# Gated recurrence of a streaming encoder: one program block over thirds of the tokens, with 64-row products of head pairs

## The chip, the core and the metric

The kernel runs on one core of one Trainium2 chip. Five engines work side by side and are tied together by semaphores: TensorE (PE in the rows; its weight loads are PEld), VectorE (DVE), ScalarE (ACT), GpSimd (POOL) and SyncE (SP), which here issues the DMA transfers. Products go into PSUM, eight banks of 512 fp32 columns on 128 partitions. The metric is device time in microseconds of one execution; less is better.

## What is computed

A trunk of two layers for 1024 prompt frames and 32 sample frames (1056 tokens). The part in question is head group A of layer 0, gated linear attention with 4 heads, 64 key and 128 value dimensions:

```python
loga = log_sigmoid(lr @ w_a2 + b_a) / 16                 # (T, 4 heads, 64)
# per chunk:  b = cumsum(loga) in the chunk
att   = einsum('thd,shd,tshd->hts', q, k, exp(b_t - b_s)) # causal, s <= t
o     = att @ v + (q * exp(b)) @ S
S_new = S * exp(b_last) + (k * exp(b_last - b)).T @ v
# then per head:  o = rmsnorm(o, onorm) * silu(g), and o goes into the output projection
```

The prompt starts with S = 0, the sample with a given state. Both last states are outputs.

## The kernel before

All tensors lie transposed: features on partitions, tokens along the free dimension (`TOK` = 1056 columns). A chunk is `C` = 32 tokens, so there are `NCH` = 33 chunks: 32 of the prompt (`NPC`), one of the sample. `BLK` is a third of the tokens, 352 columns or 11 chunks. Two heads share the 128 partitions of a pair (64 key dimensions each), so q, k and the gate are two tiles `a` of 128 partitions.

`even_layer` (L2941) runs, one after the other, program blocks that each end with all engines meeting: `front`, `even_products` (the input projection, which leaves q, k, v, g and the gate in DRAM), then for group A

- `gla_prep` (L455): loads everything whole (1056 columns), ScalarE and VectorE form log-sigmoid, the cumulated sum per chunk (a scan that the tile `keep` restarts every 32 columns), exp(c/16) as `t` and exp(-c/16) as `l`; then q*t and k*l, each written twice with a mask that keeps one head of the pair (`of_key`), and the decays `dec`.
- `gla_scan` "p" (L93) for 32 chunks, then `gla_scan` "s" for the sample's chunk. Per chunk GpSimd copies k and q into padded tiles `kp`, `qp` (L142; per pair 128 columns, of which the heads' 32 each are filled) and v into `vst` (L147). TensorE transposes `kp` and `vst` (L165, L166), forms kp.qp (L172, 128 by 128, both pairs summed into one bank), kt.vt for the state (L183), state.qp (L187) and vt.g (L190) for the output. VectorE masks (L209), adds to and decays the state (L213, L217). ScalarE empties the transposes (L229, L231) and the output (L235).
- `gla_post` (L520): per head over all 1056 columns: square (L562), column sums through a product with ones (L550), ln (L571) and exp (L574) for 1/rms, silu of g (L576), and on VectorE the gain (L583) and the gate (L587). After each the function table of ScalarE may be loaded anew (ACT_TABLE_LOAD).

Then `after_mixer` starts with the output projection's weights (L879) and everything downstream, which is untouched.

The order inside `gla_scan` comes from `staggered`: `ahead(c+1)` before `body(c)` on PE, DVE and ACT. What ties the loop: GpSimd may refill `qp` only after the output of the chunk before the last has left the array, since

```python
pe.wait_ge(y_done, c + 1)      # L191, end of scan(c) on PE
pe.sem_inc(used, 1)            # L192
pool.wait_ge(used, c + 1)      # L149, before heads(qp, q, q_padded)
```

and `make` waits for `q_padded` before L172. A product of fp32 operands is two passes on TensorE, so one product counts as x2 in the trace's rows.

## Time and profile before

| what | us |
|---|---|
| time, median of 3 runs | 3828.34 |
| lowest, highest | 3823.66, 3831.31 |
| the profiled execution's own time | 3826.76 |
| its span | 3825.0 |
| PE busy in it | 3488.0 (91%) |
| DVE, ACT, POOL busy | 1557.2, 1140.9, 602.9 |

The span runs from the first to the last instruction of the program; the 1.8 us between span and time lie around it. PE's share says little about one stage: in the page's 40 slices PE is at 9 tenths or more in most, and at 5 to 8 in a few, among them the fifth to the seventh (383 to 669 us), where group A lies.

### The profile page before, as it was taken

The numbers are of one execution on the slowest core, as the hardware profiler recorded it, in microseconds if no ns is written. First come the engines' busy times: TensorE is split into PE (matmuls) and PEld (weight loads), VectorE is DVE, ScalarE is ACT, GpSimd is POOL, SyncE is SP. The second block draws the span as 40 slices with busy tenths as digits, with TensorE's granted clock in tenths as the row PEclk, the third lists the DMA queues.
The fourth block names the chain that finished last, engine by engine and source line by source line (L and its number), as shares of the span: only waits on it lengthen the run. The fifth ranks groups of instructions, "written<-read, shape, count | busy, mean of one in ns | idle before, by whom it ended". The sixth has DMA issues, their size and how long they took to land. (4 is left out here: it accounts for less than half of the span.)

```text
span 3825.0 us, 61773 instructions
## 1 busy us (share of the span) xinstructions
PE 3488.0 (91%) x26489; PEld 3283.9 (86%) x26489; DVE 1557.2 (41%) x2522; ACT 1140.9 (30%) x2121; POOL 602.9 (16%) x859
## 2 busy tenths in 40 slices
PE   8899586999999999998899894775999999999998
PEld 8898465998999999996598784673998999999997
DVE  6345433334332232235326658456334332232233
ACT  6223225223321121124535521443323321121123
POOL 2000040101110010111312347330200210010012
PEclk9999797999999999998899997887999999999999
DMA  7322202200211111113646665965210111111111
GB/s 228 98 64 61 85 4 64 83 28 28 45 49 45 45 47 48 45 42 113 220 153 207 225 171 120 228 147 119 70 46 23 45 45 50 45 45 50 45 41 67
DMA packets 453966, 323.63 MB, mean 85 GB/s; under 512 B 105038, under 2 KB 429870, under 8 KB 450446
## 3 DMA queue, kind: packets, MB, share of 16 engines
q1 hardware_dynamic: 399450, 281.18, 25.7%
q10 hardware_dynamic: 43876, 18.99, 1.9%
q0 software_dynamic: 10368, 19.51, 1.6%
q8 instruction: 210, 3.44, 0.4%
q14 instruction: 62, 0.51, 0.0%
HBM read 232.75 MB, written 86.96 MB: 84 GB/s over the span
## 5 line engine op out<-in xcount | busy, mean ns | idle before, releaser
L83 PE MATMUL ps<-am_y,am_wh 128*128 128x352 f32 x4896 | 1178.0, 322 | 0.0
L83 PE MATMUL ps<-am_h,am_wh 128*128 128x352 f32 x3648 | 879.2, 324 | 1.2 <-DVE am_h L1379 1.2
L83 PEld LDWEIGHTS ps<-am_y,am_wh 128*128 128x128 f32 x4896 | 853.6, 188 | 1.3
L83 PE MATMUL ps<-am_y,am_wl 128*128 128x352 f32 x2448 | 789.7, 323 | 0.0
L83 PEld LDWEIGHTS ps<-am_h,am_wh 128*128 128x128 f32 x3648 | 632.1, 188 | 4.2 <-DVE am_h L1379 1.4
L83 PE MATMUL ps<-am_h,am_wl 128*128 128x352 f32 x1824 | 585.0, 321 | 0.0
L83 PEld LDWEIGHTS ps<-am_y,am_wl 128*128 128x128 f32 x2448 | 459.8, 188 | 0.0
L83 PEld LDWEIGHTS ps<-am_h,am_wl 128*128 128x128 f32 x1824 | 342.1, 188 | 0.0
L1466 POOL TENSOR_TENSOR am_silu<-am_silu,rs 128x352 f32<-128x352 f32 x132 | 126.4, 959 | 1234.4 <-ACT am_silu L1323 1234.4
L83 PE MATMUL ps<-rw_parts,rw_wh 128*128 128x352 f32 (+1 forms) x1152 | 289.3, 333 | 23.0 <-PEq L2494 13.1
L1055 DVE TENSOR_TENSOR x<-ps,x 128x352 f32<-128x352 f32 x240 | 125.8, 524 | 449.8 <-PE ps L83 439.9
L887 ACT ACTIVATE am_wh<-am_w 128x1024 fp32r<-128x1024 f32 (+1 forms) x184 | 189.4, 1030 | 377.0 <-PE ps L83 370.1
L894 DVE TENSOR_TENSOR am_wl<-am_w,am_wh 128x1024 fp32r<-128x1024 f32 (+1 forms) x184 | 222.6, 1210 | 161.6 <-ACT am_wh L887 161.6
L997 POOL TENSOR_TENSOR am_q_acc<-am_q_acc,am_q_sq 128x352 f32<-128x352 f32 x126 | 120.1, 953 | 790.2 <-ACT am_q_sq L988 790.2
L83 PE MATMUL ps<-h,ab_wh 128*128 128x352 f32 x912 | 222.7, 326 | 10.9 <-DVE ab_wl L894 10.9
L83 PEld LDWEIGHTS ps<-rw_parts,rw_wh 128*128 128x128 f32 x1152 | 202.7, 191 | 33.4 <-issue 27.1
L1438 DVE TENSOR_TENSOR am_silu<-ps,rs 128x352 f32<-128x352 f32 x132 | 69.2, 525 | 326.2 <-PE ps L83 306.8
L83 PE MATMUL ps<-rw_parts,rw_wl 128*128 128x352 f32 (+1 forms) x576 | 188.3, 327 | 0.0
L1327 ACT ACTIVATE am_h<-am_q_sq 128x352 fp32r<-128x352 f32 x132 | 65.8, 498 | 395.1 <-DVE am_q_sq L1444 395.1
L1323 ACT ACTIVATE am_silu<-am_silu 128x352 f32<-128x352 f32 x132 | 65.4, 498 | 385.3 <-DVE am_silu L1438 385.3
L83 PEld LDWEIGHTS ps<-h,ab_wh 128*128 128x128 f32 x912 | 159.1, 189 | 18.7 <-DVE ab_wl L894 11.1
L1444 DVE TENSOR_TENSOR am_q_sq<-ps,am_silu 128x352 f32<-128x352 f32 x132 | 69.2, 524 | 217.4 <-PE ps L83 217.4
(345 smaller groups left out, 4676.0 us busy)
## 6 DMA issues: line engine op xcount, KB each, us to landing
am_w<-in_ffn_w SPq DMA_DIRECT2D x120, 512.0 KB, 3.9
rw_ra_d<-tb_rk SPq DMA_DIRECT2D x8, 1056.0 KB, 8.0
rw_kbt_d<-tb_gk SPq DMA_DIRECT2D x8, 1056.0 KB, 4.0
rw_gg_d<-tb_gk SPq DMA_DIRECT2D x8, 1056.0 KB, 6.6
fr_w<-in_xa_wk SPq DMA_DIRECT2D x8, 1024.0 KB, 5.3
fr_w<-in_xa_wv SPq DMA_DIRECT2D x8, 1024.0 KB, 5.3
am_w<-in_xa_wq SPq DMA_DIRECT2D x16, 512.0 KB, 4.0
am_w<-in_xa_wo SPq DMA_DIRECT2D x16, 512.0 KB, 4.0
```

Source lines behind the costliest of these rows:

```text
L83: mm = nc.tensor.matmul(out, l, part, start=start and n == 0, stop=stop and n == 2)
L887: self.nc.scalar.activation(self.wh[:, j % 2, 0:kt], self.wt[:, j % 2, 0:kt], ACT.Copy)\
L894: self.nc.vector.tensor_tensor(self.wl[:, j % 2, 0:kt], self.wt[:, j % 2, 0:kt], whole(self.wh[:, j % 2, 0:kt]), ALU.subtract).then_inc(se ...
L997: self.nc.gpsimd.tensor_tensor(acc, acc, self.sq[:, n % 2], ALU.add).then_inc(self.added, 1)
L1055: g.frees(g.nc.vector.tensor_tensor(xs, g.bank(j, b), xs, ALU.add), j, b)
L1323: nc.scalar.activation(silu[:, columns(b)], silu[:, columns(b)], ACT.Silu).then_inc(silus, 1)
L1327: nc.scalar.activation(z[0][:, i, columns(b)], gate[:, (f + b) % 2], ACT.Copy).then_inc(highs, 1)
L1438: groups.frees(nc.vector.tensor_tensor(silu[:, columns(b)], groups.bank(j, b), rs[:, columns(b)], ALU.mult), j, b)
L1444: groups.frees(nc.vector.tensor_tensor(gate[:, (f + b) % 2], groups.bank(j + 1, b), silu[:, columns(b)], ALU.mult), j + 1, b)
L1466: nc.gpsimd.tensor_tensor(silu[:, columns(b)], silu[:, columns(b)], rs[:, columns(b)], ALU.mult)\
```

## The change

The three blocks `gla_prep`, `gla_scan` (twice) and `gla_post` become one block `gla`. In it:

- preparation goes by thirds: block b+1 of 352 columns is loaded, and its log-sigmoid (`soft`), sums (`cumulate`), exponentials (`grow`) and products (`queries` on VectorE, k*l on GpSimd) stand at fixed chunks of block b: on ScalarE after chunk 1 and 5 of a block, on VectorE after 3 and 6. `q` isn't scaled any more, the factor moves into the copy that takes the output out.
- `qp` and `kp` exist for all 33 chunks, 64 columns per pair, zeroed once; GpSimd's per-chunk copies are gone, and each third's q*t and k*l are written straight into them, a head (64 partitions) at a time.
- products of a head pair lie on 64 rows: kp.qp (L211 in the new file) is two products of 64 by 64, each on its half of rows and partitions; kv.kv (L221) takes 64 rows of each half and 128 columns; state.qp (L230) has 128 rows and 64 moving columns; kv.g (L234) 64 rows, 64 moving columns. The two transposes (L204, L205) share a bank, one copy (L365) empties it, with two banks in turn.
- the state is double (`old`, `new`), so adding doesn't overwrite what state.qp reads; the sample is chunk 32 of the same loop with states 2 and 3.
- norm and gate of third b-1 stand at fixed chunks of third b: square after chunk 0, sum and ln of one head after chunks 1 to 4, exp after 6, silu after 7 on ScalarE; gain and gate after 8 and 9 on VectorE. Those of the last third come after the loop, a head at a time.

The core of the diff (new lines; removed functions are those described above):

```diff
+            def make(c):
+                s, b = c % 2, c // PB
+                if c % PB == 0:
+                    pe.wait_ge(vr_set, b + 1)
+                    pe.wait_ge(kp_set, 2 * b + 2)
+                if c >= 2:
+                    pe.wait_ge(kv_out, c - 1)
+                nc.tensor.transpose(ps[:, A + s, 0:P], kp[:, c].rearrange("r p h t -> r (p h t)"), ident[:])
+                nc.tensor.transpose(ps[:, A + s, P:2 * P], vr[:, c].rearrange("r h t -> r (h t)"), ident[:]).then_inc(turned, 1)
+                if c % PB == 0:
+                    pe.wait_ge(qp_set, 2 * b + 2)
+                if c:
+                    pe.wait_ge(g_out, c)
+                for p, r in enumerate(halves):
+                    mm = nc.tensor.matmul(ps[r, G, 0:HD], kp[:, c, p].rearrange("r h t -> r (h t)"),
+                                          qp[:, c, p].rearrange("r h t -> r (h t)"), start=True, stop=True)
+                mm.then_inc(made, 1)
+
+            def scan(c):
+                s = c % 2
+                pe.wait_ge(kv_out, c + 1)
+                if c:
+                    pe.wait_ge(s_added, c)
+                for p, r in enumerate(halves):
+                    mm = nc.tensor.matmul(ps[:, S + p, 0:GLA_DV], kv[r, s, 0, :], kv[r, s, 1, :], start=True, stop=True)
+                mm.then_inc(s_done, 1)
+                if c == NPC:
+                    pe.wait_ge(init_in, 32)
+                else:
+                    pe.wait_ge(state_ready, c + 1)
+                if c:
+                    pe.wait_ge(y_out, c)
+                for p in range(2):
+                    nc.tensor.matmul(ps[:, Y + p, 0:HD], state[:, old(c), p, :], qp[:, c, p].rearrange("r h t -> r (h t)"),
+                                     start=True, stop=False)
+                pe.wait_ge(g_out, c + 1)
+                for p, r in enumerate(halves):
+                    mm = nc.tensor.matmul(ps[:, Y + p, 0:HD], kv[r, s, 1, :], g[r, s, :], start=False, stop=True)
+                mm.then_inc(y_done, 1)
...
+            for b in range(BLOCKS):
+                s = b % 2
+                pool.wait_ge(v_in[s], 16 * (b // 2 + 1))
+                if b == 0:
+                    pool.wait_ge(cleared, 2)
+                nc.gpsimd.tensor_copy(vr[:, chunks(b)].rearrange("p c h t -> p h c t"),
+                                      v[:, s].rearrange("p h (c t) -> p h c t", t=C)).then_inc(vr_set, 1)
+                pool.wait_ge(grown, 2 * b + 2)
+                nc.gpsimd.tensor_copy(dec[:, :, chunks(b)], by_chunk(t[:, s])[:, :, :, C - 1]).then_inc(dec_set, 1)
+                pool.wait_ge(qk_in[s], 32 * (b // 2 + 1))
+                pool.wait_ge(dec_set, b + 1)
+                for h, r in enumerate(halves):
+                    if h:
+                        pool.wait_ge(kp_set, 2 * b + 1)
+                    nc.gpsimd.tensor_tensor(kp[r, chunks(b), :, h, :].rearrange("r c p t -> r p c t"), by_chunk(k[r, s]), by_chunk(l[r, s]), ALU.mult)\
+                        .then_inc(kp_set, 1)
...
+            for c in range(NCH):
+                if c + 1 < NCH:
+                    masked(c + 1)
+                add(c)
+                b, r = c // PB, c % PB
+                if b + 1 < BLOCKS:
+                    if r == 3:
+                        cumulate(b + 1)
+                    if r == 6:
+                        queries(b + 1)
+                if b and r == 8:
+                    if b == 1:
+                        dve.wait_ge(gain_in, 16)
+                    dve.wait_ge(scales, b)
+                    norm(b - 1, 0, GLA_HEADS)
+                if b and r == 9:
+                    dve.wait_ge(normed, b)
+                    dve.wait_ge(gated, b)
+                    bend(b - 1, 0, GLA_HEADS).then_inc(done, 1)
...
         with nc.cleanup_on_exit():
-            with nc.sbuf_tensor("gla_qk", [P, 2, 2, 2, TOK], F32) as qk, nc.sbuf_tensor("gla_v", [P, 4, TOK], F32) as v:
-                q, k = qk[:, 0], qk[:, 1]
-                gla_prep(nc, ab, gate, q, k, v, dec, a["c_keep"], a["c_heads"])
-                gla_scan(nc, ps, "p", 0, NPC, q, k, v, a["c_mask_gla"], dec, ya, None,
-                         o["p_gla"][0, 0], ident)
-                gla_scan(nc, ps, "s", NPC, 1, q, k, v, a["c_mask_gla"], dec, ya, a["state_gla"][0, 0],
-                         o["s_gla"][0, 0], ident)
-            gla_post(nc, ps, ab, ya, a["gla_onorm"][0], ones)
+            gla(nc, ps, a, o, ab, gate, ya, ones, ident)
```

What stands in the queues. On PE, in the middle of the loop before, one chunk is these rows (x2: two products, one per pair):

```order
L165 MATMUL ps<-ident,glap_kp 128x128 x2
L166 MATMUL ps<-ident,glap_vst 128x128
L172 MATMUL ps<-glap_qp,glap_kp 128x128 x2
L183 MATMUL ps<-glap_vt,glap_kt 128x128 x2
L187 MATMUL ps<-glap_qp,glap_state 128x128 x2
L190 MATMUL ps<-glap_g,glap_vt 128x128
```

and in the changed kernel, same place:

```order
L204 MATMUL ps<-ident,gl_kp 128x128
L205 MATMUL ps<-ident,gl_vr 128x128
L211 MATMUL ps<-gl_qp,gl_kp 64x64 x2
L221 MATMUL ps<-gl_kv 128x128 x2
L230 MATMUL ps<-gl_qp,gl_state 128x64 x2
L234 MATMUL ps<-gl_gm,gl_kv 128x64 x2
```

One transpose fewer, one product kv.g more, and fewer moving columns in three groups (L211, L230, L234); L211, L221 and L234 take 64 rows of the array, the others 128.

On ACT, the preparation before stands whole (2112 columns: both tiles of 1056 tokens) ahead of the first chunks' copies:

```order
L484 ACTIVATE gp_t<-gp_z 128x2112
L486 ACTIVATE gp_l<-gp_t 128x2112
L489 ACTIVATE gp_t<-gp_l,gp_one 128x2112
L492 ACTIVATE gp_t<-gp_c 128x2112
L493 ACTIVATE gp_l<-gp_c 128x2112
L495 ACTIVATE gla_dec<-gp_t 128x66
```

and in the changed kernel, around the first chunks of the second third:

```order
L365 ACTIVATE gl_kv<-ps 128x256
L370 ACTIVATE o_a<-ps 128x4x32
L378 ACTIVATE gl_sq<-o_a 128x1408
L365 ACTIVATE gl_kv<-ps 128x256
L370 ACTIVATE o_a<-ps 128x4x32
L384 ACTIVATE gl_rs<-ps,gl_eps 128x352
L349 ACTIVATE gl_t<-gl_z 128x704
L351 ACTIVATE gl_l<-gl_t 128x704
L355 ACTIVATE gl_t<-gl_l,gl_one 128x704
L365 ACTIVATE gl_kv<-ps 128x256
L370 ACTIVATE o_a<-ps 128x4x32
L384 ACTIVATE gl_rs<-ps,gl_eps 128x352
```

A chunk has two copies (L365, L370) where the loop before has three (L229, L231, L235), and between them now stand the squares (L378) and ln (L384) of the first third and `soft` (L349 to L355) of the last. Later in the same queue stand five ACT_TABLE_LOAD inside the loop: before silu, ln, exp, silu and the closing preload.

## Rows read from the trace of the kernel before

**Rows 1.** Busy time by stage: stretch (us), length, engines' busy us (instructions), PEclk, DMA.

```profile
438.00:478.00 40.00, 0.00 (x0) 0.00 (x0) 17.63 (x8) 10.00 (x6) 0.10 (x1) 0.50 0.38 149
478.00:572.00 94.00, 77.23 (x544) 64.79 (x544) 36.78 (x97) 26.56 (x96) 39.92 (x163) 0.95 0.01 3
572.00:582.00 10.00, 4.26 (x17) 3.67 (x17) 1.14 (x3) 0.83 (x3) 1.90 (x8) 0.67 0.13 34
582.00:618.00 36.00, 14.18 (x24) 7.28 (x24) 10.31 (x8) 30.25 (x27) 0.18 (x4) 0.59 0.18 60
```

**Rows 2.** Timeline, the preparation: start, us, instruction, x count [idle before <- releaser].

```profile
438.13 0.38 SPq L468 DMA_DIRECT2D gp_z<-gla_gate_t  x1
...
449.90 1.96 ACT L484 ACTIVATE gp_t<-gp_z 128x2112 f32<-128x2112 f32 x1 [21.11 <-DMA gp_of_key<-in_c_heads]
...
458.37 4.61 DVE L506 TENSOR_TENSOR_SCAN gp_c<-gp_keep,gp_z 128x1056 f32<-128x1056 f32 x2
...
479.80 0.69 PE L165 MATMUL ps<-ident,glap_kp 128*128 128x128 f32 x2 [45.70 <-POOL glap_vst L147]
```

**Rows 3.** DMA issues of the preparation: KB, median us to landing.

```profile
gla_v<-ab_t SPq DMA_DIRECT2D x1, 2112.0 KB, 14.3
...
gp_z<-gla_gate_t SPq DMA_DIRECT2D x1, 1056.0 KB, 5.0
```

**Rows 4.** Timeline, one chunk of the prompt's loop.

```profile
560.48 0.64 POOL L142 COPY glap_qp<-gla_qk 128x64 f32<-128x64 f32 x2 [1.45 <-PEq L192]
...
561.07 0.41 POOL L142 COPY glap_kp<-gla_qk 128x64 f32<-128x64 f32 x2
...
561.17 0.71 PE L172 MATMUL ps<-glap_qp,glap_kp 128*128 128x128 f32 x4
...
561.72 0.61 PE L183 MATMUL ps<-glap_vt,glap_kt 128*128 128x128 f32 x4
...
562.17 0.61 PE L187 MATMUL ps<-glap_qp,glap_state 128*128 128x128 f32 x4
...
562.82 0.42 DVE L213 TENSOR_TENSOR glap_state<-ps,glap_state 128x256 f32<-128x256 f32 x1 [0.60 <-PE ps L187]
563.04 0.28 ACT L235 ACTIVATE o_a<-ps 128x128 f32<-128x128 f32 x1 [1.30 <-PE ps L190]
563.16 0.64 POOL L142 COPY glap_qp<-gla_qk 128x64 f32<-128x64 f32 x2 [1.45 <-PEq L192]
```

**Rows 5.** Timeline, norm and gate, and the start of the next stage.

```profile
589.38 1.28 ACT L576 ACT_TABLE_LOAD   x1
...
590.68 1.08 ACT L576 ACTIVATE go_g<-go_g 128x1056 f32<-128x1056 f32 x1
...
615.54 1.26 DVE L587 TENSOR_TENSOR o_a<-o_a,go_g 128x1056 f32<-128x1056 f32 x1 [1.14 <-ACT go_g L576]
617.79 3.89 SPq L879 DMA_DIRECT2D am_w<-in_ab_w_out  x6
```

**Rows 6.** Timeline of PE, small products elsewhere (cross-attention, layer 1's scan).

```profile
798.84 0.97 PE L1197 MATMUL ps<-xpt,xmem 128*128 128x32 f32 x8
...
2509.85 0.64 PE L327 MATMUL ps<-ds_state,ds_ra 128*64 128x64 f32 x16
2510.31 0.64 PE L334 MATMUL ps<-ds_ra,ds_state 128*64 128x64 f32 x16
2510.88 0.69 PE L367 MATMUL ps<-ds_z,ds_tt 64*64 64x64 f32 x32
```

**Rows 7.** POOL's groups of instructions: busy us, mean ns, idle before.

```profile
L997 POOL TENSOR_TENSOR am_q_acc<-am_q_acc,am_q_sq 128x352 f32<-128x352 f32 x126 | 120.1, 953 | 790.2 <-ACT am_q_sq L988 790.2
...
L132 POOL MEMSET glap_kp<- 128x512 f32 x1 | 0.5, 525 | 0.0
```

**Rows 8.** Timeline of POOL beside two long VectorE instructions in layer 1.

```profile
2258.57 2.75 POOL L1912 TENSOR_TENSOR x<-x 88x112 f32<-88x112 f32 x1
```

**Rows 9.** Busy time by stretch in layer 1's scan, columns as in Rows 1.

```profile
2535.00:2545.00 10.00, 7.61 (x210) 6.75 (x208) 4.45 (x13) 4.64 (x8) 3.58 (x7) 0.84 0.88 198
```

More of the change, by code:

```diff
@@ L116, in _ @@
+        four = lambda r, b: ab[r:r + 4 * P, columns(b)].rearrange("(h p) t -> p h t", p=P)
+        halves = (slice(0, HD), slice(HD, P))
+        old, new = (lambda c: 2 if c == NPC else c % 2), (lambda c: 3 if c == NPC else (c + 1) % 2)
+        by_chunk = lambda t: t.rearrange("r p (c t) -> r p c t", t=C)
+        chunks = lambda b: slice(b * PB, (b + 1) * PB)
         @block.sync
         def _(sp):
-            sp.dma_start(mask[:], mask_d).then_inc(mask_in, 16)
-            if state_in is not None:
-                for h in range(2):
-                    sp.dma_start(state[HD * h:HD * h + HD], state_in.rearrange("(p h) a b -> h a p b", h=2)[h])\
-                        .then_inc(init_in, 16)
@@ new lines, in _ @@
+            init = a["state_gla"][0, 0].rearrange("(p h) a b -> h a p b", h=2)
+            for h, r in enumerate(halves):
+                sp.dma_start(state[r, 2], init[h]).then_inc(init_in, 16)
+            load(1)
+            sp.dma_start(gain[:], a["gla_onorm"][0].rearrange("(p o) -> p o", o=1)).then_inc(gain_in, 16)
+            load_g(0)
+            load_g(1)
+            load(2)
+            load_g(2)
+            sp.wait_ge(state_ready, NPC + 1)
+            store(0, new(NPC - 1))
+            sp.wait_ge(state_ready, NPC + 2)
@@ new lines, in total @@
+            def total(b, h, bank):
+                if h == 0:
+                    pe.wait_ge(squares, b + 1)
+                if b < BLOCKS - 1 and (b or h):
+                    pe.wait_ge(logs, GLA_HEADS * b + h)
+                nc.tensor.matmul(ps[:, bank, 0:BLK], ones[:], sq[:, h], start=True, stop=True).then_inc(sums, 1)
+            make(0)
+            for c in range(NCH):
+                if c + 1 < NCH:
+                    make(c + 1)
+                scan(c)
+                b, r = c // PB, c % PB
+                if b and 1 <= r <= GLA_HEADS:
+                    total(b - 1, r - 1, TOTAL)
@@ L219, in _, with cumulate @@
-            staggered(dve, n, make, scan)
+            def cumulate(b):
+                s = b % 2
+                dve.wait_ge(act_step, 3 * b + 3)
+                nc.vector.scalar_tensor_tensor(out=zz[:, s], in0=zz[:, s], scalar=0.0, in1=t[:, s], op0=ALU.min,
+                                               op1=ALU.subtract).then_inc(z_set, 1)
+                dve.wait_ge(z_set, b + 1)
+                if b == 0:
+                    dve.wait_ge(keep_in, 16)
+                for p in range(2):
+                    nc.vector.tensor_tensor_scan(c_[:, s, p], keep[:], zz[:, s, p], 0.0, ALU.mult, ALU.add).then_inc(cums, 1)
@@ L238, in _, with square @@
-            staggered(act, n, make, scan)
+                nc.scalar.activation(y[:, :, c * C:(c + 1) * C].rearrange("r (p h) t -> r p h t", h=2),
+                                     ps[:, Y:Y + 2, 0:HD].rearrange("r p (h t) -> r p h t", h=2), ACT.Copy,
+                                     scale=GLA_DK ** -0.5).then_inc(y_out, 1)
+            def square(b, h0, h1):
+                act.wait_ge(y_out, min(NCH, PB * (b + 1)))
+                if b:
+                    act.wait_ge(sums, GLA_HEADS * b)
+                nc.scalar.activation(sq[:, h0:h1], y[:, h0:h1, columns(b)], ACT.Square).then_inc(squares, 1)
```

402 lines of the change are left out of this document (169 added, 233 removed).

## Prediction

> **What bounds the kernel now.** I read the busy time by stage first [rows 1]. Group A's four stages take 438 to 618 us. TensorE is idle in the whole preparation, busy 77.2 of 94 us in the prompt's loop and 14.2 of 36 us in norm and gate. These 179.7 us (438.13 [rows 2] to 617.79 [rows 5]) are a latency chain between full meetings of the engines, and nothing of another stage lies beside them. So what the new block saves, the kernel saves. The next view is the timeline of each stage.
>
> Preparation: the first activation waits for all loads until 449.90, the last product ends before 478, and PE starts at 479.80, 41.7 us after the first DMA [rows 2].
>
> Loop: GpSimd's copy of q starts at 560.48 and again at 563.16, so a chunk is 2.68 us [rows 4]. The chain is seen there: copies of q 0.64, then L172 from 561.17, L183 from 561.72, L187 from 562.17, kv.g behind it, then 1.45 us of GpSimd's wait ends when the output has left PE. Two passes stand 0.11 us apart ((562.17 - 561.72) / 4) when nothing holds them; the first one after a wait costs 0.10 more (0.71 against 0.61 for four).
>
> Norm and gate: ScalarE is busy 30.3 of 36 us [rows 1], with table loads of 1.28 [rows 5] between its steps.
>
> **The change, part by part.** All against the profiled execution (span 3825.0, own time 3826.8; the median is 3828.3, so I subtract the saving from the median).
>
> *Start to first transpose: 14.7 us instead of 41.7.* Gate, 352 columns: the whole gate landed in 5.0 us and 5.8 MB in about 17 (v is issued 2.7 us in and takes 14.3) [rows 3], so a third of it lands after 2.1 to 5.0; I take 3.0. ScalarE: 2112 columns cost 1.96 [rows 2] and 1056 cost 1.08 [rows 5], which makes 0.84 us per 1000 columns plus 0.2, so 0.80 for 704 and 2.4 for the three of `soft`. VectorE: 1.26 for 1056 [rows 5], 0.42 for 256 [rows 4], so 0.95 for the 704 of `cumulate`, and 4.61 / 6 = 0.8 for each of its two scans: 2.6 to 2.8. Both exponentials 1.6. That is 448.0. GpSimd meanwhile zeroes 2 x 4224 columns: 512 cost 0.525 [rows 7], so 7.2 to 8.7, and copies v; both end by then. k*l on GpSimd: 953 ns for 352 columns [rows 7], 1.7 to 1.9 for 704, two of them 3.4 to 3.8. It also gets held by VectorE's `queries` (2 x 0.9): in [rows 8] 112 columns took 2.75 us beside two VectorE instructions of 1056 columns or so, and in the loop the pair of copies takes 0.64 beside the decay L217 and 0.41 without [rows 4]. First transpose at 438.1 + 14.7 = 452.8. Between 13 and 18.
>
> *First products.* `make(0)`, `make(1)` and the first mask stand alone: 1.6 us, and PE comes to them at its lower level (granted 0.50, 1.2 GHz, in the idle preparation [rows 1]): 2.0 more.
>
> *A chunk on PE: 1.98 us instead of 2.68.* Passes: two transposes 0.22. kp.qp: 64-column products overlap in [rows 6], 16 passes from 2509.85 to 2510.31, 0.029 each, and the 64 by 64 ones run faster still (32 in 0.69 with their latency): 0.12. state.qp: 64 moving columns save nothing, since 8 passes with 32 moving columns and 128 weight columns still stood 0.10 apart (0.97 less the last one's 0.28, by 7) [rows 6]: 4 x 0.112 = 0.45. kv.kv and kv.g: two products of 64 rows and 128 columns, on different rows. No row has such a pair. Bounds: fully overlapped 0.22 each, as the 64 by 64 products in [rows 6], or one after the other 0.45 each. I take 0.22, because L367 overlaps over rows as well as columns. Sum 1.23.
>
> To this come five changes of array shape per chunk (128x128, 64x64, 64x128, 128x128, 64x128 and back), which the old loop doesn't have. In [rows 6] L334 (128*64) holds PE 0.57 us until L367 (64*64) starts, L327 of the same count only 0.46: 0.11 lost ahead of a change. Behind it the weight load is bare, 0.05 (half of the 0.10 above) to 0.10. I take 0.15 for each change: 0.75. Sum 1.98; bounds 1.23 plus nothing, and 0.9 + 1.55 = 2.43 with serial pairs.
> The Trainium skill says it too (TensorEngine Tiling (Array Packing), Tiling Modes, Key Properties): a change of tiling mode drains TensorE; by that rule, the 0.11 agrees.
>
> *Other loops around a chunk.* Adding and decaying the state: kv.kv's last pass ends 0.5 after its first, add 0.42, decay 0.42, semaphores 0.1: 1.5 after kv.kv starts, and state.qp of the next chunk is due 2.4 after it. Output: state.qp to end of kv.g about 1.0, copy 0.28 [rows 4], 0.1: 1.4 of 1.98. So PE binds, and a step put between chunks may hold ScalarE about 1.7 us and VectorE about 1.75 before PE waits.
>
> *Steps between chunks.* `soft` 2.4 costs 0.7, `soft` with an ln (2.95) 1.25. Table load plus 1408 or 1056 columns (1.28 + 1.37) costs 0.95, four times; with an ln 0.1. Squares, exponentials and the bare exp of 1408 columns (1.37): nothing. Sum on ScalarE 5.9. VectorE: `cumulate` 2.8 costs 1.05, twice; `queries`, gain, gate (1.6 to 1.8): nothing. GpSimd's k*l of the next third has 7.5 us from its exponentials to the border and needs 3.8, plus about 3.1 of being held: 1 us late in all. On PE eight sums with ones of 352 columns, 0.6 each: 4.8. Together 13.8.
>
> *Clock.* Old loop 0.95 [rows 1], its slow first us included; layer 1's scan, with small products too and PE busy 7.6 of 10, is granted 0.84 [rows 9]. I add 3 us.
>
> *Tail.* Square, sum, ln, exp, then four heads on ScalarE at 1.0 each and the squares, gain and gate of the last: 8.1, and 1.0 to the next stage (615.54 + 1.26 to 617.79 [rows 5]). The stores and the landing of the states (gone from the chain: about 3 us each before) lie beside it.
>
> Sum: 14.7 + 3.6 + 33 x 1.98 (65.3) + 13.8 + 3 + 9.1 = 109.5 us instead of 179.7: 70 us less, **3758**. The rest of the kernel starts as before: weights asked for at its first instruction, PE at the lower level.
>
> **The rivals.**
> - *Pairs on 64 rows don't overlap* (so far the change doesn't do what it says). 33 x 0.45 = 14.9 more, and a longer chunk hides some 4 of the steps: 3769. For it: no row with 128 weight columns side by side. Chance 0.17.
> - *Shape changes cost little*, because their cost lies in a wait. A chunk is then bound by the output's loop, 1.35: 33 x 0.63 = 20.8 less, but slack falls by 0.6 and the steps cost 8 more: 3745. Chance 0.13.
> - *The clock stays low.* PE is granted 0.50 whenever it idles [rows 1], and the new loop uses half the rows and stalls at steps. Passes double, 33 x 1.23 = 41 more, steps and clock term shrink by 10, sums double by 2: 3791. Against it: the old loop ran at full clock with 0.6 us gaps. Chance 0.06. The Trainium skill (TensorE: Matmul & The Clock Gate, Part 4) says that transposes don't count as activity, which would be for it; no row here parts the two.
> - *Table loads cost more than their row.* ScalarE would stand 1.4 longer at each of five loads, 6.9 us: 3765. Against it: 589.38 + 1.28 and silu starts at 590.68 [rows 5]. Chance 0.04. That longer price is the rule of the Trainium skill (ScalarE: Activation LUTs, What ACT_TABLE_LOAD costs: about 2.66 us with the drain); the row differs.
> - *Slower than before: GpSimd's k*l.* Each third hangs on two products in a four-dimensional pattern, with VectorE's two-input instructions holding GpSimd. At [rows 8]'s factor of six a product is 10.5 us instead of 1.7: 53 more, less 8 hidden, 3803. It decides from 13 us each (6 x 11.7 = 70); at 15 the time is 3838. Chance 0.02, and 0.04 for the milder sort near 3803.
>
> **How the numbers follow.** Forecast as worked out, give or take 12: 0.51. The rest as above, 0.03 for what I don't see, most of it still faster. The range takes the forecast, the serial pairs, the cheap changes and the table loads, 0.85 together: 3734 to 3782. A measurement of this kernel tells about 0.2% (8 us) from no change. Faster by more than that 0.97, the same 0.01, slower 0.02.
>
> **What the profile would show.** Right: first transpose of `kp` near 452.8, 33 chunks about 2.0 apart with PE not waiting, pairs of L221 starting within 0.01 us, 0.1 us holes at each change of shape, and the output projection's weights asked for near 548. Serial pairs show as four starts 0.11 apart. The low clock shows as 0.50 in the loop's stretch and a chunk of 3.2. A GpSimd limit shows as PE waiting for k*l (`kp`) at chunks 11 and 22. Wrong would be a chunk bound by another wait (ScalarE's output copy above all) or a first third later than 456.

## The result

| what | us |
|---|---|
| time after, median of 4 runs | 3792.35 |
| lowest, highest | 3789.96, 3795.6 |
| time before, median of the 4 runs beside them | 3829.82 |
| the profiled execution's own time, its span | 3794.63, 3792.7 |

The ratio is 0.9907, 95% interval 0.9894 to 0.9919: faster by 0.9%, about 37 us. The forecast was 3758 with a range of 3734 to 3782, so the saving is about half of what was forecast (37 of 70 us) and the time lies outside the range. It is within 1.4 us of the rival *the clock stays low* (3791), which had a chance of 0.06.

The profile after, busy time by stage (stretch, length, busy us and instructions of PE, PEld, DVE, ACT and POOL, then the granted clock as a share of 2.4 GHz and DMA), as [rows 1]:

```profile
core 0: us, PE busy (x) PEld busy (x) DVE busy (x) ACT busy (x) POOL busy (x), PEclk, DMA share, GB/s
438.00:454.00 16.00, 0.34 (x2) 0.29 (x2) 5.47 (x6) 5.21 (x6) 13.72 (x9) 0.52 0.95 300
454.00:577.00 123.00, 121.76 (x605) 87.36 (x603) 55.53 (x112) 45.24 (x94) 10.10 (x8) 0.50 0.08 27
577.00:589.00 12.00, 6.83 (x15) 3.09 (x14) 5.01 (x10) 7.92 (x15) 0.00 (x0) 0.50 0.07 17
```

Preparation and tail are what the plan wanted: 16 us instead of 40, and 12 instead of 46 (10 of these 46 were the sample's own scan, which is now chunk 32 of the loop). The loop is the surprise. It takes 123 us where the old one took 94, TensorE is busy in 121.76 of them, and it runs at 0.50, that is 1.2 GHz, from the first chunk to the last. The old loop had 0.95. Here is where the old one rose, 6 us after its first product (columns as above):

```profile
482.00:486.00 4.00, 3.70 (x18) 3.35 (x17) 1.14 (x3) 0.83 (x3) 0.68 (x4) 0.50 0.00 0
486.00:490.00 4.00, 3.67 (x29) 3.17 (x29) 1.43 (x4) 1.38 (x5) 2.02 (x10) 1.00 0.00 0
```

Timeline after, the start (start, us, instruction, x count, idle before and its releaser), beside [rows 2]:

```profile
441.57 0.79 ACT L349 ACTIVATE gl_t<-gl_z 128x704 f32<-128x704 f32 x1 [1.84 <-DMA gl_z<-gla_gate_t]
...
449.56 3.96 POOL L191 TENSOR_TENSOR gl_kp<-gl_k,gl_l 64x704 f32<-64x704 f32 x2 [0.15 <-POOL gl_dec L185]
...
453.66 0.45 PE L204 MATMUL ps<-ident,gl_kp 128*128 128x128 f32 x1 [19.25 <-POOL gl_kp L191]
```

Timeline of PE after, one chunk, beside [rows 4]. It ends with the next chunk's first row:

```profile
558.87 0.42 PE L204 MATMUL ps<-ident,gl_kp 128*128 128x128 f32 x1
...
559.43 0.48 PE L211 MATMUL ps<-gl_qp,gl_kp 128*64 128x64 f32 x4
...
559.85 0.80 PE L221 MATMUL ps<-gl_kv 64*128 64x128 f32 x4
...
560.58 1.11 PE L230 MATMUL ps<-gl_qp,gl_state 128*128 128x64 f32 x4
...
561.62 0.69 PE L234 MATMUL ps<-gl_gm,gl_kv 64*128 64x64 f32 x4
562.25 0.47 PE L204 MATMUL ps<-ident,gl_kp 128*128 128x128 f32 x1
```

No row here carries an idle time: PE waits for nobody, it is slow. This stretch is 3.38 us; most of the 32 distances between first transposes are 3.43, those with a sum 4.71, the first is 1.0 (chunks 0 and 1 are started together), and all together are 118.9 (453.66 to 572.52).

The end of the part after, beside [rows 5]:

```profile
577.53 0.69 PE L234 MATMUL ps<-gl_gm,gl_kv 64*128 64x64 f32 x4
577.63 1.28 ACT L417 ACT_TABLE_LOAD   x1
...
578.92 0.28 ACT L370 ACTIVATE o_a<-ps 128x128 f32<-128x128 f32 x1
...
587.55 0.52 DVE L304 TENSOR_TENSOR o_a<-o_a,gl_g 128x352 f32<-128x352 f32 x1
589.09 0.38 SPq L895 DMA_DIRECT2D am_w<-in_ab_w_out  x1
```

Group A takes 438.45 to 589.09, 150.6 us instead of 179.7: 29 saved. The span fell by 32.3; the rest of the program is 3.6 shorter (589.09 to 3792.7 against 617.79 to 3825.0), less than that rest differs among the runs below.

### The profile page after: what moved, and what is told of

Same layout as the page of the kernel before. It is cut to its first block and busy times, and to the rows that moved or that the text cites. A ratio compares the mean times of both kernels' runs of the same rounds, so it can differ in the third digit from the quotient of the medians.

```text
span 3792.7 us, 61595 instructions
## 1 busy us (share of the span) xinstructions
PE 3515.1 (93%) x26522; PEld 3294.5 (87%) x26522; DVE 1554.9 (41%) x2533; ACT 1131.8 (30%) x2104; POOL 584.8 (15%) x704
```

## The experiments

The question was why a loop in which TensorE is never idle stays at 1.2 GHz. Four theories:

- **Start.** The loop could hold 2.4 GHz, it only never gets there.
- **Rows**, or **columns**, or both. Its passes carry less than the old ones: kv.kv and kv.g use 64 of 128 rows, kp.qp 64 weight columns, three of five groups move 64 columns instead of 128. The passes of state.qp are no shorter for it, so the same busy time holds less work.
- **More products** on PE, of any kind, would lift it (the sums with ones are long and full).
- **Shape changes** in themselves make the chunk long, whatever the clock.

The pitch is the distance of the first transposes of two chunks, "loop" that from chunk 0 to chunk 32. One run each except where an interval is given, so most rows show the clock of a single execution.

| kernel | pitch at 1.2 / 2.4 GHz | clock in the loop | loop | time |
|---|---|---|---|---|
| after | 3.43 / - | 0.50 throughout | 118.9 | 3792.4 |
| e1_warm | 3.43 / 2.01 | 1.00 to 478, then 0.50 | 111.6 | 3808.3 |
| e8_warm17 | 3.43 / - | 0.50 from 454 on | 118.9 | 3799.2 |
| e2_rows128 | 3.59 / 1.97 | 0.50 until 520 | 109.6 | 3786.5 |
| e3_wide_y | 3.53 / 2.07 | 0.50 until 517 | 107.1 | 3784.2 |
| e7_filler | 4.71 / - | 0.50 throughout | 147.0 | 3818.4 |
| e4_block | 3.04 / 1.72 | 0.50 until 497 | 89.6 | 3774.4 |
| e9_dense | 3.05 / 1.68 | 0.50 until 505 | 88.9 | 3774.9 |
| e10_dense_warm | 3.05 / 1.68 | 0.50 from 454 until 502 | 91.2 | 3769.7 |
| e14_columns | 3.64 / 2.12 | 0.50 until 506 | 108.2 | 3776.0 |
| e5_full | 3.6 / 1.99 | 1.00 from 462, with two falls | 80.8 | 3755.1 |
| e6_full_warm | - / 1.99 | 1.00 throughout | 74.1 | 3751.9 |
| e13_rows_wide | 3.59 / 1.97 | 1.00 from 460, with one fall in the loop | 79.3 | 3753.5 |
| e11_dense_full | - / 1.95 | 1.00 from 460 to the end | 73.8 | 3753.6 |
| e12_dense_full_warm | - / 1.95 | 1.00 until 457 and from 460 to the end | 73.1 | 3753.6 |
| e15 (e11 again) | - / 1.95 | 1.00 from 460 to the end | 73.8 | 3753.9 |

The loop column says more than the time. What follows group A, which no edit touches, took 3196.6 us (e14) to 3212.5 us (e4 and e9) in these profiles, and the kernel before had medians of 3828.7 to 3832.6 beside the other runs but 3837.8, in its only run, beside e4 to e7. So a few microseconds of total time between two rows mean nothing.

**First call: a warm start, full rows, full columns.**

e1_warm: 40 products ahead of `make(0)`.

```diff
+            for _ in range(40):
+                nc.tensor.matmul(ps[:, TOTAL, 0:BLK], ones[:], x[:, 0, 0:BLK], start=True, stop=True)
             make(0)
```

> TensorE gets 40 extra fp32 products (ones by 352 columns of x, into the unused bank 7) in front of the loop's first transpose; the stretch 438 to 453 us, where it is idle, takes them (80 passes of about 0.15 us at 2.4 GHz, 0.3 at 1.2, so 12 to 24 us, which may end up to 9 us after the first transpose would be due). Theory 'the level is held, not reached' (the loop only lacks a start at 2.4 GHz, as the old loop reached 1.00 by itself): the granted clock in 460 to 590 us is 1.00 or near it, a chunk takes 2.0 to 2.4 us instead of 3.42, and the time is 3792 less 33 to 45 us, 3747 to 3759, plus what the extra products run over. Theory 'the loop's products themselves pull the level down' (64 rows, 64 columns): the clock starts at 1.00 and is back at 0.50 within some chunks, a chunk is 3.42 again, and the time is 3785 to 3800.

Measured: 3808.28 median of 4, ratio to before 0.9943 (0.9927 to 0.996). The extra products ran 12 us too far (first transpose at 465.62). Windows, then one chunk at 2.4 GHz:

```profile
458.00:476.00 18.00, 17.56 (x116) 12.07 (x115) 5.62 (x15) 5.43 (x13) 0.00 (x0) 1.00 0.26 90
480.00:500.00 20.00, 18.86 (x102) 13.66 (x100) 10.99 (x18) 5.21 (x14) 5.53 (x4) 0.50 0.00 1
```

```profile
470.31 0.33 PE L204 MATMUL ps<-ident,gl_kp 128*128 128x128 f32 x1
...
470.68 0.34 PE L211 MATMUL ps<-gl_qp,gl_kp 128*64 128x64 f32 x4
470.95 0.49 PE L221 MATMUL ps<-gl_kv 64*128 64x128 f32 x4
471.37 0.66 PE L230 MATMUL ps<-gl_qp,gl_state 128*128 128x64 f32 x4
...
471.96 0.44 PE L234 MATMUL ps<-gl_gm,gl_kv 64*128 64x64 f32 x4
...
472.33 0.33 PE L204 MATMUL ps<-ident,gl_kp 128*128 128x128 f32 x1
```

The chunk is 2.01 us at the upper level: the forecast's 1.98 was right for a clock that the kernel doesn't get. And *start* falls: 13 us into the loop the level was lost, in the second of two chunks in which PE waits behind the preparation of the next third (0.41 us for ScalarE at 473.44, 0.27 for VectorE at 477.55), and for the 100 us of loop that followed it didn't come back. e6 below waits in the same chunks and keeps the level.

e2_rows128: kv.kv and kv.g contract over all rows, which mixes the pairs, so its states and outputs are not those of the kernel.

```diff
-                    mm = nc.tensor.matmul(ps[:, S + p, 0:GLA_DV], kv[r, s, 0, :], kv[r, s, 1, :], start=True, stop=True)
+                    mm = nc.tensor.matmul(ps[:, S + p, 0:GLA_DV], kv[:, s, 0, :], kv[:, s, 1, :], start=True, stop=True)
...
-                    mm = nc.tensor.matmul(ps[:, Y + p, 0:HD], kv[r, s, 1, :], g[r, s, :], start=False, stop=True)
+                    mm = nc.tensor.matmul(ps[:, Y + p, 0:HD], kv[:, s, 1, :], g[:, s, :], start=False, stop=True)
```

> kv.kv (L221) and kv.g (L234) contract over all 128 rows instead of 64, so the two heads of a pair are mixed in the state and the output (that part of the computation is changed; the count of products and columns is not). Theory 'half the rows is what keeps the clock low': the granted clock rises to 1.00 some chunks into the loop, as in the kernel before, and a chunk is 2.0 to 2.4 us; time about 3755. Theory 'small moving counts and gaps, not rows': 0.50 through the whole loop, a chunk 3.3 to 3.5 us, time 3788 to 3796. Theory 'shape changes are dear': at the same 0.50 a chunk gets shorter by up to 4 x 0.15 = 0.6 us for the changes that fall away, less 0.2 to 0.4 if the 64-row pairs had overlapped: 3.0 to 3.3, time 3780 to 3788.

e3_wide_y: state.qp moves 128 columns, of which 64 are used.

```diff
+                flat = qp[:].rearrange("r c p h t -> r (c p h t)")
                 for p in range(2):
-                    nc.tensor.matmul(ps[:, Y + p, 0:HD], state[:, old(c), p, :], qp[:, c, p].rearrange("r h t -> r (h t)"),
+                    w = HD if p and c % PB == PB - 1 else P
+                    at = (2 * c + p) * HD
+                    nc.tensor.matmul(ps[:, Y + p, 0:w], state[:, old(c), p, :], flat[:, at:at + w],
```

> state.qp (L230) takes 128 moving columns instead of 64 (the other 64 are the neighbouring pair's and are never read; at the end of a third one product keeps 64). Theory 'too few moving columns keeps the clock low': the granted clock in the loop rises above 0.50 and a chunk falls from 3.42 towards 2.2; time 3755 to 3770. Theory 'a product is bound by its weight load, and the clock looks at something else': still 0.50, chunk 3.42 to 3.50, time 3792 to 3796. If 64 columns did save time over 128 after all, a chunk is up to 0.4 us longer: 3805.

Measured: 3786.49 and 3784.21. Neither alone lifts the clock in the first third. In both it rises behind the sums with ones of the second third (chunks 12 to 15), which in the changed kernel did nothing, and falls again 7 and 10 us later (e2 520.4 to 527.2, e3 517.4 to 527.6). Beside the sums of the last third it rises once more, for 17 us in each. The windows up to the first rise, e2 first:

```profile
458.00:518.00 60.00, 59.02 (x281) 50.16 (x281) 26.10 (x53) 18.52 (x43) 5.52 (x4) 0.50 0.04 15
```

```profile
458.00:514.00 56.00, 55.07 (x269) 38.41 (x268) 25.69 (x52) 18.08 (x42) 5.53 (x4) 0.50 0.04 15
```

e2 also answers *shape changes*. One of its chunks at 2.4 GHz:

```profile
521.83 0.71 PE L221 MATMUL ps<-gl_kv 128*128 128x128 f32 x4
522.37 0.56 PE L230 MATMUL ps<-gl_qp,gl_state 128*128 128x64 f32 x4
522.77 0.61 PE L234 MATMUL ps<-gl_gm,gl_kv 128*128 128x64 f32 x4
523.21 0.28 PE L204 MATMUL ps<-ident,gl_kp 128*128 128x128 f32 x1
```

From kv.kv to the next chunk it is 1.38 us with no change of shape, and 1.38 in e1 (470.95 to 472.33) with three. The rows tell where it went: L221 holds PE 0.42 us in e1 and 0.54 in e2, L234 0.37 and 0.44, but L230, which stands between two changes in e1 and between none in e2, 0.59 and 0.40. So the pairs do overlap somewhat, and the changes of shape give it back. At 1.2 GHz e2's chunk is 0.16 longer than after's, not shorter. Working on 64 rows bought next to nothing at 2.4 GHz and 0.16 at 1.2, which is also the end of *shape changes* as the cause of the long chunk.

**Second call: fuller passes and more products.**

e4_block: one product kv.g for both pairs (g block-diagonal, 128 rows, 128 columns) ahead of state.qp, in one bank.

```diff
+                pe.wait_ge(g_out, c + 1)
+                nc.tensor.matmul(ps[:, Y, 0:P], kv[:, s, 1, :], g[:, s, :], start=True, stop=False)
                 for p in range(2):
-                    nc.tensor.matmul(ps[:, Y + p, 0:HD], state[:, old(c), p, :], qp[:, c, p].rearrange("r h t -> r (h t)"),
-                                     start=True, stop=False)
-                pe.wait_ge(g_out, c + 1)
-                for p, r in enumerate(halves):
-                    mm = nc.tensor.matmul(ps[:, Y + p, 0:HD], kv[r, s, 1, :], g[r, s, :], start=False, stop=True)
+                    mm = nc.tensor.matmul(ps[:, Y, p * HD:(p + 1) * HD], state[:, old(c), p, :],
+                                          qp[:, c, p].rearrange("r h t -> r (h t)"), start=False, stop=p == 1)
```

> The output keeps one bank for both pairs, as in the kernel before: kv.g becomes one product of 128 rows and 128 moving columns with a block-diagonal g (bank zeroed once), first in its group, and state.qp follows into its 64 columns each. Two passes stand where four of 64 rows stood, two changes of array shape fewer; 20 of the 22 passes' work is the same. By the passes' rows of the first runs a chunk is 1.75 to 1.85 us at 2.4 GHz and 3.0 to 3.1 at 1.2. Theory 'the granted clock follows how much of the array and of the time moves columns' (the first three runs: 64-row chunks at 64 columns fall back, fuller ones rise where the sums with ones are): somewhat fuller than the changed kernel, about like the run with 128 moving columns, so 0.50 at first and 1.00 in part of the stretches with sums: time 3770 to 3782. Theory 'the level depends on nothing in the chunk' (chance where it rises): 0.50 throughout, 3780 from the shorter chunk alone.

Measured: 3774.37. The pitch is as expected at 1.2 GHz and a little shorter at 2.4 (1.72 against 1.75 to 1.85). The clock rose at 497, beside the first sums; some of the gain is only the shorter chunk.

e5_full: state.qp and kv.g of each pair with 128 moving columns, kv.g on 128 rows with a block-diagonal g. As in e4, state.qp now also waits for g.

```diff
+                pe.wait_ge(g_out, c + 1)
                 for p in range(2):
-                    nc.tensor.matmul(ps[:, Y + p, 0:HD], state[:, old(c), p, :], qp[:, c, p].rearrange("r h t -> r (h t)"),
+                    nc.tensor.matmul(ps[:, Y + p, 0:P], state[:, old(c), p, :], qp[:, c].rearrange("r p h t -> r (p h t)"),
                                      start=True, stop=False)
-                pe.wait_ge(g_out, c + 1)
-                for p, r in enumerate(halves):
-                    mm = nc.tensor.matmul(ps[:, Y + p, 0:HD], kv[r, s, 1, :], g[r, s, :], start=False, stop=True)
+                for p in range(2):
+                    mm = nc.tensor.matmul(ps[:, Y + p, 0:P], kv[:, s, 1, :], g[:, s, :], start=False, stop=True)
```

> As before, but each pair has its bank and both products there have 128 moving columns: state.qp moves both pairs' q, kv.g the whole block-diagonal g, and the copy reads 64 columns of each bank. The passes are again 22, 16 of them now on 128 rows and 128 columns. At 2.4 GHz a chunk is 2.0 us, at 1.2 GHz 3.4 to 3.5. Theory 'columns and rows in motion': at the lower level the chunk is about 0.7 full instead of 0.5 of the changed kernel, above the run that rose only beside sums; the clock rises within 30 us of the first chunk and stays, time 3755 to 3770. Theory 'nothing but the sums with ones lifts it' (both rises of the first runs came beside them): 0.50 until 500 us at least, then as in the wide run, time 3780 to 3790.

Measured: 3755.1, 37 us under the changed kernel with the same 18 passes a chunk (two transposes of one pass and four groups of four in the rows; the expectations count four too many, here and for e9 and e11). Windows before and behind the rise:

```profile
454.00:458.00 4.00, 2.22 (x14) 1.36 (x16) 0.35 (x2) 0.77 (x2) 3.00 (x2) 0.50 1.06 365
...
462.00:478.00 16.00, 13.81 (x124) 11.19 (x122) 12.43 (x24) 7.65 (x19) 3.63 (x3) 1.00 0.04 13
```

In the second row PE is busy 13.81 of 16 us, at 1.00. In the changed kernel it is busy nearly all the time (121.76 of 123 us), at 0.50. The profile's busy share doesn't tell which level a loop will have. The Trainium skill (TensorE: Matmul & The Clock Gate, What's actually happening) lets the clock follow how busy PE has been; by the busy share of the profile alone, this row and the changed kernel's contradict it. The share of weight loads (PEld) doesn't tell either: it is 50.16 of 60 us in e2 at 0.50, and was 3.35 of 4 where the old loop rose.

e6_full_warm: e5 with 17 products with ones ahead.

> The full kernel of the run before plus 17 products with ones (34 passes) in the idle stretch ahead of the first transpose, which end before it (in the first warm run the passes took 0.6 us each for 4 us and 0.3 us after). Theory 'columns and rows in motion': 1.00 from the first chunk on and held, with short falls at most, a chunk of 2.0 and one with a sum of 2.7: time 3750 to 3760, some 15 us under the same kernel without them if that one rises late. Theory 'only a long stretch of wide products holds it': 1.00 for 25 us as in the first warm run, then 0.50: 3775 to 3785.

Measured: 3751.91, 1.00 from 443 to 535 and a loop of 74.1 against e5's 80.8. A fall in the loop as e5's did not occur.

e7_filler: a product with ones (352 columns) behind each chunk that has no sum.

```diff
+                else:
+                    n = b if r > GLA_HEADS else b - 1
+                    if n > 0:
+                        pe.wait_ge(logs, GLA_HEADS * n)
+                    nc.tensor.matmul(ps[:, TOTAL, 0:BLK], ones[:], x[:, 0, 0:BLK], start=True, stop=True)
```

> The changed kernel with one product of ones by 352 columns of x added after every chunk that has no sum (result never read), so that PE does more work: 25 products, 50 passes. Theory 'columns in motion': each chunk is then like those with a sum, the clock goes to 1.00 early in the loop and stays; 33 chunks of 2.70 (as measured with a sum at 2.4 GHz) instead of 25 of 3.42 and 8 of 4.71: 123 down to 90 us, so 3760 to 3768, faster with more work. Theory 'the level has nothing to do with what PE does': 33 chunks of 4.71, 155 us, 3822 to 3827.

Measured: 3818.42. 31 distances of 4.7 behind the first, and no rise:

```profile
454.00:602.00 148.00, 148.00 (x634) 100.14 (x636) 50.71 (x108) 44.85 (x92) 10.31 (x8) 0.50 0.07 23
```

So *more products* falls, and with it the simple form of my own theory, which had promised 3760 to 3768. A full product behind each thin chunk lifted nothing; behind fuller ones (e2, e3, e4) the clock rose.

**Third call: a short warm start, a denser chunk.** e8_warm17 is the changed kernel with 17 products ahead; e9_dense adds to e4 a single product kp.qp for both pairs; e10_dense_warm is e9 with the 17 products.

```diff
-                for p, r in enumerate(halves):
-                    mm = nc.tensor.matmul(ps[r, G, 0:HD], kp[:, c, p].rearrange("r h t -> r (h t)"),
-                                          qp[:, c, p].rearrange("r h t -> r (h t)"), start=True, stop=True)
-                mm.then_inc(made, 1)
+                nc.tensor.matmul(ps[:, G, 0:P], kp[:, c].rearrange("r p h t -> r (p h t)"),
+                                 qp[:, c].rearrange("r p h t -> r (p h t)"), start=True, stop=True).then_inc(made, 1)
```

> The changed kernel, its own chunks, with 17 products of ones in the idle stretch ahead (they end before the first transpose, unlike the 40 of the first warm run). Theory 'the thin chunks can't hold the level': 1.00 from about 444 us, first transpose on time at 454, back to 0.50 after 10 to 25 us of loop, the next 23 or more chunks at 3.42: 8 to 12 chunks gain 1.4 us each, time 3776 to 3784. Theory 'the level, once reached before the loop and without the 12 us delay, is kept': 3745 to 3755.

> The block-diagonal output of e4 and, besides, kp.qp of both pairs as one product of 128 rows, 128 weight columns and 128 moving columns (2 passes instead of 4 of 64 columns; what the pairs give crosswise is zeroed by the mask). 18 passes instead of 22, nearly all on the whole array, two changes of shape fewer again. By the rows of e4 (1.72 us at 2.4 GHz, 3.04 at 1.2) and 0.20 to 0.27 for the two passes in place of 0.27 plus a change: 1.60 to 1.70 and 2.8 to 2.95. Theory 'fullness of the passes': fuller than e4, near the full kernel, so the clock rises within the first third: time 3742 to 3760. Theory 'moving counts of state.qp alone decide it' (the full kernel was the one with 128 there): as e4, 0.50 until 495 us, time 3765 to 3772.

> The dense kernel with the 17 warm-up products. Theory 'fullness of the passes': 1.00 from the first chunk and mostly held, chunk 1.6 to 1.7, steps between chunks cover more of it, so 70 us for the loop against 74 of the full warm kernel (3752): 3742 to 3750, ratio to the kernel before about 0.978. If the level falls at a step as it did once in the full warm kernel, 5 to 10 us more: 3752 to 3758.

Measured: 3799.23, 3774.93, and 3769.74 (3763.13 to 3776.32, ratio 0.9838, 0.9824 to 0.9853). All three are slower than expected. The level was lost near the first transpose (windows: e8 in steps of 1 us, e8 in steps of 4, e10):

```profile
453.00:454.00 1.00, 0.00 (x0) 0.00 (x0) 0.00 (x0) 0.00 (x0) 0.99 (x1) 1.00 1.08 352
454.00:455.00 1.00, 0.18 (x1) 0.21 (x2) 0.00 (x0) 0.00 (x0) 0.94 (x2) 0.50 1.06 366
```

```profile
450.00:454.00 4.00, 1.74 (x6) 0.76 (x4) 1.38 (x2) 0.00 (x0) 3.77 (x3) 1.00 1.07 362
454.00:458.00 4.00, 3.18 (x18) 2.09 (x19) 0.74 (x3) 0.77 (x2) 2.04 (x2) 0.50 1.06 368
```

```profile
450.00:454.00 4.00, 0.77 (x6) 0.64 (x6) 0.15 (x2) 0.33 (x1) 3.86 (x3) 1.00 1.07 362
454.00:458.00 4.00, 3.76 (x19) 3.10 (x20) 1.49 (x5) 1.10 (x4) 0.51 (x1) 0.58 1.06 368
```

PE had stood idle 3.08 and 3.52 us ahead of the first transpose. In e8 the clock fell in this gap: it is 0.50 from 454.0 on, 0.8 us ahead of the first transpose at 454.82 and 2.3 behind the last product with ones. So e8 doesn't show what its chunks would have held. In e10 it fell at 454.7, 1.5 us into the loop. In e6 PE stood idle 2.95 us and the level stayed, so the gap's length alone doesn't tell either. e9 shows that fewer and full passes don't do it alone: its pitch is no shorter than e4's at 1.2 GHz (3.05 against 3.04), half of state.qp's columns still don't move, and the clock rose no earlier than in e4 (505 against 497). The five runs of e10 spread over 13 us, so a single run's time can be off by several microseconds.

**Fourth call: both.** e11_dense_full has e5's output products and e9's kp.qp; e12 adds 20 products ahead.

> The full output products of e5 (two banks, 128 moving columns in state.qp and kv.g) together with e9's single kp.qp product: 20 passes, 16 on the whole array with 128 moving columns, 4 on 64 rows in pairs. From e9's chunk (1.68 at 2.4 GHz, 3.05 at 1.2) and two more passes of 0.112 or 0.213: 1.90 and 3.48. Theory 'the chunk's fullness': the fullest so far, so the clock rises no later than in e5 (about 460 us) and falls less often (e5: three times): loop 70 to 76 us against 80.8, time 3742 to 3752. Theory 'e5 rose by luck of when the chip looks': 0.50 until 495 us at least as in e4 and e9: 3768 to 3780.

> The same with 20 products of ones ahead, so that they reach to the first transpose (17 ended at 451.7 us in two runs, and the level was gone at 454 there). Theory 'fullness': 1.00 at the first chunk and kept, loop 68 to 72 us, time 3738 to 3748, ratio to the kernel before about 0.976. If a gap of 2 us ahead of the first transpose decides whether the warm-up lasts, it lasts here; if it is chance, it may fall at once and come back within 10 us, 3744 to 3752.

Measured: 3753.63, and 3753.6 (3749.23 to 3754.39, ratio 0.9797, 0.9775 to 0.982). Both times lie above what fullness had promised (3742 to 3752, 3738 to 3748), but both have 1.00 from 460 to the loop's end with not one fall (here e11):

```profile
462.00:526.00 64.00, 60.81 (x466) 50.74 (x465) 45.21 (x96) 36.72 (x81) 11.28 (x7) 1.00 0.04 13
```

In e12 PE stood idle 1.5 us ahead of the first transpose, the level reached before the loop was lost near 457 and back at 460, and the loop is 73.1 against 73.8: here the products ahead bought nothing that the time shows.

**Fifth call: rows against columns, and a repetition.** e13_rows_wide is e2's and e3's edits together; like e2 it mixes the pairs, so its states and outputs are not those of the kernel. e14_columns is e5 with kv.g back on 64 rows:

```diff
-                for p in range(2):
-                    mm = nc.tensor.matmul(ps[:, Y + p, 0:P], kv[:, s, 1, :], g[:, s, :], start=False, stop=True)
+                for p, r in enumerate(halves):
+                    mm = nc.tensor.matmul(ps[:, Y + p, 0:P], kv[r, s, 1, :], g[r, s, :], start=False, stop=True)
```

> The edits of e2 and e3 together, on the changed kernel: kv.kv and kv.g on all 128 rows (which mixes the pairs, so state and output are changed; the count of passes is not) and state.qp with 128 moving columns. Chunk by their rows 2.0 us at 2.4 GHz, 3.6 at 1.2. Each alone stayed at 0.50 until the sums with ones. Theory 'rows and columns add up': both together lift the clock within the first third, time 3750 to 3765. Theory 'it needs kv.g with 128 moving columns': 0.50 until about 515 us, 3782 to 3788.

> The full kernel e5 with kv.g back on 64 rows, two at a time, but with 128 moving columns each: so all columns are full and only rows differ from e5, in this one product. A chunk is 3.4 to 3.5 us at 1.2 GHz, 2.0 at 2.4. Theory 'rows and columns add up': the two 64-row products side by side fill the array as one does, only for half as long; fuller than e3, thinner than e5: 0.50 in the first third, 1.00 beside the sums and longer than in e3, time 3765 to 3782. Theory 'columns decide, rows don't': clock up at 460 as in e5, 3752 to 3758.

> The same kernel as e11, to give its time an interval: 3750 to 3757 and a ratio to the kernel before of 0.979 to 0.981 if its clock rises near 460 us in every run; if the rise depends on chance, single runs near 3770 would show.

Measured: e13 3753.49, e14 3775.95, e15 3753.87 (3743.82 to 3754.39; ratio to before 0.9794, 0.9781 to 0.9808). Windows of e13 and e14:

```profile
462.00:502.00 40.00, 36.57 (x314) 30.91 (x310) 27.96 (x58) 21.61 (x50) 8.55 (x6) 1.00 0.00 1
```

```profile
458.00:504.00 46.00, 45.23 (x220) 30.90 (x218) 21.44 (x41) 12.85 (x32) 5.52 (x4) 0.50 0.05 15
```

This closes the square. Full rows alone (e2): 0.50 in the first third. Full columns of state.qp alone (e3): 0.50. Both (e13): 1.00 from 460. All columns of the output products full but kv.g on 64 rows (e14): 0.50, which also refutes *columns decide*. Each corner is one execution, but the loops are 107 to 110 us against 79, and the runs of one kernel never lay more than 13.2 us apart.

What the square shows is unequal. e2 and e13 differ in state.qp's moving columns alone, so the columns count. The edits that fill the rows also take changes of shape out: a chunk has five in the changed kernel, e3 and e14, three in e5, two in e2, e13 and e11. Few changes alone don't lift the clock (e2, and e9 with two), but the runs don't part full rows from fewer changes where the columns are full. How the chip forms the level from what the passes do is in no row.

e15, which is e11 again, had no run above 3754.4 (and one of 3743.8, below its forecast, unexplained), so the rise is no luck of one profile. Its median is 0.979 of the kernel before, against 0.991 for the change as made: the version to keep.

## Why the prediction was wrong, point by point

**The failing step is the paragraph *Clock*.** It took the new loop for one that runs at the upper level like the old one, put the old loop's 0.95 and layer 1's 0.84 together and added 3 us. The measured price is 3.43 less 2.01, 1.4 us for each of 32 chunks, 45 us, and the loops of the changed kernel and of e6, 118.9 and 74.1, differ by as much. What I had was that the new loop "uses half the rows", and I set against it that the old loop ran at full clock with gaps of 0.6 us. That argument is about time in which PE is idle. The runs show that the make-up of the passes matters: with fuller passes and more idle time (e5, e13) the level is 1.00 for most of the loop, with thin ones and hardly any idle time it is 0.50. Of the sum's 109.5 us for group A the rest held up: kernels that have the level which it assumed take 105.3 (e6, with the changed kernel's kp.qp and kv.kv and a pitch of 1.99; and e11) to 111.5 us (e5, with two falls). The changed kernel itself never ran its whole loop at that level, so 3758 is made likely by these, not measured.

**The rival *clock stays low* had the mechanism**: 3791, measured 3792.4. That the totals lie 1.4 us apart is partly luck. By the rival group A takes 142.5 us (109.5 and 33 more), and it took 150.6; the rest of the program happened to be 3.6 shorter, and the rest of the difference lies between the profiled executions and the medians. Its chunk of 3.2 was 3.43, as the time around changes of shape grew at the lower clock too; against that, its steps shrank more than the 10 us allowed, being hidden nearly whole by the long chunk.

**Start to first transpose, 14.7**: measured 15.2 (438.45 to 453.66), with `soft` at 0.79, 0.79 and 0.88 and k*l at 3.96 for two, as forecast. Right. One term was misread: the prediction's own two rows (1.26 for 1056 columns, 0.42 for 256) give 0.89 for 704, not 0.95, and 0.89 was measured.

**A chunk, 1.98**: measured 2.01 at 2.4 GHz in e1, right as a sum, by errors that cancel. The pairs overlap less than I took: 0.207 for the pair with 128 moving columns and 0.153 with 64, instead of 0.11. The changes of shape cost 0.05 to 0.1 instead of 0.15. I had also described kp.qp as 64 by 64 on half of the rows. The rows say `128*64`: it uses all 128 rows and 64 weight columns. The section on the change has it wrong in the same way.

**Steps between chunks, 13.8**: in the changed kernel nearly nothing, since a chunk of 3.43 covers them. The sums cost 1.28 each at 1.2 GHz and 0.60 at 2.4 (e11: 2.55 less 1.95), the latter as forecast. The largest stall was not on the list. It is `queries` behind chunk 6. Its first product takes 2.35 us beside GpSimd's k*l of the same third, its second 1.94 beside the copy of v (alone such a product takes 0.89); the mask for chunk 8 comes late and kp.qp of chunk 9 waits for it (timeline after, POOL, DVE and PE):

```profile
477.40 3.48 POOL L191 TENSOR_TENSOR gl_kp<-gl_k,gl_l 64x704 f32<-64x704 f32 x2
...
479.28 4.32 DVE L278 TENSOR_TENSOR gl_qp<-gl_q,gl_t 64x704 f32<-64x704 f32 x2
...
480.95 1.91 POOL L182 COPY gl_vr<-gl_v 128x1408 f32<-128x1408 f32 x1
...
483.90 0.48 PE L211 MATMUL ps<-gl_qp,gl_kp 128*64 128x64 f32 x4 [1.14 <-DVE gl_gm L283]
```

I had given `queries` 1.6 to 1.8 for the two and no price; the price is 1.2 (a distance of 4.65 instead of 3.43). At full clock it is 2.0 in e6 (4.01 less 1.99) and 0.7 in e11 (2.64 less 1.95), where both start ahead of k*l and take 0.88 and 0.89. At full clock (e11) the loop is 73.75: 32 x 1.95, sums 4.8, 1.2 for the first chunks at the lower level, and 5.4 for all other steps, against 9.0 forecast for them.

**Table loads**: the rival that they cost more than their row is wrong. The load takes 1.28 and the next activation starts 0.02 behind it, as [rows 5] had it:

```profile
566.08 1.28 ACT L388 ACT_TABLE_LOAD   x1
...
567.38 1.38 ACT L388 ACTIVATE gl_rs<-gl_rs 128x1408 f32<-128x1408 f32 x1
```

**Tail, 8.1 and 1.0**: 10.2 from the last output copy to the next stage (578.92 to 589.09). The copy itself came about 0.65 late, behind the closing table load at 577.63: elsewhere it starts 0.74 behind the first pass of kv.g, which would be 578.27.

**Serial pairs, GpSimd's k*l as the limit**: neither came. Pairs started 6 ns apart. k*l took 1.7 to 2.2 each, and PE waited for it nowhere behind the first chunk.

## What to carry to other kernels

Before a loop's products are made smaller, ask what that does to TensorE's clock, above all where the new loop follows an idle stretch: fewer moving columns saved state.qp no time, pairs on 64 rows saved 0.16 us of a chunk at 1.2 GHz and nearly nothing at 2.4, and with such products the clock of the whole loop was half. Read the granted clock of a loop next to its busy time; TensorE was busy nearly all the time here, at 0.50, and filling its output products with columns that nobody reads and rows that add zero (e5) made this kernel 1.0% faster with the same number of passes (one run; e11 with its repetition gained as much). Warm-up products ahead of the loop were no cure for the thin loop: in e1 the level was lost 13 us into the loop, in e8 before it began, and in neither did it come back.

## What the runs showed that I had not expected

- TensorE busy 148 of 148 us and granted 1.2 GHz throughout (e7), with full 352-column products in every chunk.
- An unpaired pass with 128 weight columns and 64 moving columns takes as long as one with 128: state.qp's four starts are 0.11 apart in e1 (64) and e3 (128), and at 1.2 GHz e3's chunk is only 0.1 longer.
- Two products on separate halves of the rows start 6 ns apart, yet a pair with 128 moving columns holds PE 0.207 us at 2.4 GHz, as long as nearly two full passes (0.224).
- The level once lost needn't come back: 100 us in e1, with PE busy nearly all the time.

- The falls in the loop come where PE waits. All three of e5 and e13 lie in the distance that `queries` stretches (e5 at 479.0 in one of 4.89 us and at 509.7 in one of 4.17, e13 at 504.4 in one of 5.02). In e11 these distances are 2.64 and 2.63 and it has no fall.

What stays open: why e6, with two such distances of 4.0, didn't fall; what took the level in e10 and e12 within 2 us of the first transpose; and whether full rows or fewer changes of shape were the second condition beside full columns. Whether transposes count like other products wasn't tried.
